# Query and key chunks of a q/k/v projection: five float32r products per weight tile instead of six, with a readout in two halves

## What is computed

```python
def project_qkv(h, w_qkv, q_norm, k_norm):
    b, t, _ = h.shape
    p = (h @ w_qkv).reshape(b, t, N_GROUPS, 3, H_SLOT, HEAD_DIM)
    q = rmsnorm(p[:, :, :, 0], q_norm)
    k = rmsnorm(p[:, :, :, 1], k_norm)
    v = p[:, :, :, 2]
    return q, k, v
```

## Time and profile before

| | before |
|---|---|
| median of three runs | 1206.25 us |
| profiled execution | 1206.42 us |
| its span, first to last instruction | 1204.9 us |
| mean granted TensorE clock | 0.999 of full speed |
| matmul busy (weight loads busy) | 1192.5 us, 99% (1142.0 us, 95%) |
| VectorE busy | 779.7 us, 65% |
| ScalarE busy | 544.1 us, 45% |

### The profile page before, as it was taken

One profiled execution on the slowest core, in us unless ns is written; L12 is line 12 of the kernel. 1 busy time (PEld: TensorE's weight loads), 2 busy tenths in 40 slices (PEclk: granted clock), 3 DMA queues, 4 the chain that ended last, 5 costly groups with the idle time before them and its releaser, 6 DMA issues.

```text
span 1204.9 us, 26364 instructions
## 1 busy us (share of the span) xinstructions
PE 1192.5 (99%) x10349; PEld 1142.0 (95%) x10349; DVE 779.7 (65%) x1427; ACT 544.1 (45%) x953; POOL 21.1 (2%) x50
## 2 busy tenths in 40 slices
PE   8999999999999999999999999999999999999998
PEld 8999999999999999999999999988999999999998
DVE  6766676777776644445686776768877777774333
ACT  5333345445445433224466555555654444542221
POOL 0000000000000000000000000000000000000000
PEclk9999999999999999999999999999999999999999
DMA  8355544656444545455467766668544454546542
GB/s 218 100 164 168 171 119 138 201 152 191 151 135 149 165 155 161 142 170 171 151 209 193 222 181 184 193 168 221 147 149 138 147 173 152 151 144 182 131 115 44
DMA packets 285301, 193.19 MB, mean 160 GB/s; under 512 B 40393, under 2 KB 281537, under 8 KB 284070
## 3 DMA queue, kind: packets, MB, share of 16 engines
q1 hardware_dynamic: 282092, 137.04, 41.5%
q0 software_dynamic: 1792, 54.43, 12.6%
q10 hardware_dynamic: 1338, 0.61, 0.2%
HBM read 184.52 MB, written 64.16 MB: 206 GB/s over the span
## 4 chain that ended last, share of the span: by engine, by line
PE 88%; DVE 7%; ACT 2%; issue 2%; DMA 0%; DVEq 0%; ACTq 0%
PE acc L1968 21%; PE acc L1950 15%; PE acc L1972 11%; PE acc L1969 11%; PE acc L1970 11%; PE acc L1971 11%; DVE wl L1273 1%; PE acc L1998 1%; DVE u L1744 1%; PE N L1937 1%; PE N L2242 1%; PE M L1937 1%; DVE big L1626 1%; ACT wh L872 1%; DVE skv L1737 1%
## 5 line engine op out<-in xcount | busy, mean ns | idle before, releaser
L872 ACT ACTIVATE wh<-wraw 128x1024 fp32r<-128x1024 f32 (+1 forms) x211 | 217.9, 1033 | 267.5 <-PE acc L1972 175.6
L1273 DVE TENSOR_TENSOR wl<-wraw,wh 128x1024 fp32r<-128x1024 f32 (+1 forms) x211 | 252.9, 1199 | 128.9 <-ACT wh L872 100.2
L1968 PE MATMUL acc<-h_both,wh 128*128 128x512 f32 x840 | 319.0, 380 | 2.1 <-DVE wl L1273 1.9
L1972 PE MATMUL acc<-h_both,wl 128*128 128x264 f32 x840 | 233.5, 278 | 0.0
L1970 PE MATMUL acc<-h_both,wh 128*128 128x264 f32 x840 | 231.8, 276 | 0.0
L1969 PE MATMUL acc<-h_both,wh 128*128 128x264 f32 x840 | 231.8, 276 | 0.0
L1971 PE MATMUL acc<-h_both,wl 128*128 128x256 f32 x840 | 229.0, 273 | 0.0
L1970 PEld LDWEIGHTS acc<-h_both,wh 128*128 128x128 f32 x840 | 158.8, 189 | 22.7
L1950 PE MATMUL acc<-h_both,wh 128*128 128x256 f32 x1120 | 173.4, 277 | 0.4 <-DVEq L1678 0.3
L1968 PEld LDWEIGHTS acc<-h_both,wh 128*128 128x128 f32 x840 | 161.3, 192 | 2.7 <-issue 2.2
L1969 PEld LDWEIGHTS acc<-h_both,wh 128*128 128x128 f32 x840 | 158.8, 189 | 0.0
(11 more groups left out here) (274 smaller groups left out, 1735.7 us busy)
## 6 DMA issues: line engine op xcount, KB each, us to landing
out_dram<-in_cache_kv_d_dram POOLq DMA_DIRECT2D x24, 1364.0 KB, 6.2
wraw<-in_ffn_w_gate_dram SPq DMA_DIRECT2D x44, 512.0 KB, 3.9
wraw<-in_ffn_w_up_dram SPq DMA_DIRECT2D x44, 512.0 KB, 3.9
wraw<-in_attn_w_qkv_dram SPq DMA_DIRECT2D x36, 512.0 KB, 4.2
out_dram<-in_cache_kv_d_dram POOLq DMA_DIRECT2D x8, 2044.0 KB, 8.3
wraw<-in_ffn_w_down_dram SPq DMA_DIRECT2D x32, 448.0 KB, 3.9
wraw<-in_sc_w_in_dram SPq DMA_DIRECT2D x24, 512.0 KB, 3.9
wraw<-in_ffn_w_down_dram SPq DMA_DIRECT2D x16, 512.0 KB, 4.3
```

The source lines that it names most:

```text
L872: nc.scalar.activation(wh[c % 2][:, 0:k], wraw[:, c % 4, 0:k], ACT.Copy).then_inc(hi_done, 1)
L1273: V.tensor_tensor(wl[c % 2][:, 0:k], wraw[:, c % 4, 0:k], wh[c % 2][:, 0:k].bitcast(F32), ALU.subtract).then_inc(split_done, 1)
L1968: T.matmul(wide, h[:, k, :], wide_pairs(both[:, :, k0 + k]), start=start, stop=False)
L1972: ins = T.matmul(rest, l[:, k, :], paired(high, 1, CUT), start=False, stop=stop)
```

## The change

Query and key chunks (`c % 3 < 2`, 24 of the 36) use `wide_products`. ScalarE gets a `keep_low` ahead of the split of the next weights, for each of them; it writes the low result straight into the buffer of queries and keys, and waits until the normalisation of the tile that lay there before is done. VectorE's readout first scales the columns of bank 1, then adds part 0 to the kept low result, then scales the samples, releases the banks, and scales the sum only afterwards. Value chunks stay as they were.

```diff
         IN_WIDE = 3 * (DK - 1)
-        WIDE = (IN_WIDE, IN_WIDE + 2 * FK - 4)
+        QKV_WIDE = IN_WIDE + 2 * FK
+        WIDE = (IN_WIDE, QKV_WIDE + 6 * NP_ - 4)
+
+        def prompt_tile(q):
+            return qk_t[:, q % 2, 0:SEQ].rearrange("p (h n) -> p h n", h=2)
...
             for cc in range(9 * NP_):
                 p, c = divmod(cc, 9)
                 n = (p - 1) * NCLS + (c - 1) // 2
+                if cc and (cc - 1) % 3 < 2:
+                    q = (cc - 1) // 9 * 6 + (cc - 1) % 9 // 3 * 2 + (cc - 1) % 3
+                    if q >= 2:
+                        act.wait_ge(norm_ready, q - 1)
+                    keep_low(S_QKV, 0, cc - 1, qkv_bank(cc - 1), prompt_tile(q))
                 if cc:
                     step(S_QKV, 0, cc - 1)
...
                 if c % 3 < 2:
                     q = p * 6 + 2 * g + c % 3
                     t = qk_t[:, q % 2]
-                    V.tensor_tensor(t[:, 0:SEQ].rearrange("p (h b n) -> p h b n", h=2, b=2), prompt_by_half(a),
-                                    cut2(prompt(r)), ALU.mult)
+                    n = QKV_WIDE + q + 1
+                    V.tensor_tensor(rest_set(prompt_tile(q)), rest_part(a)[:, :, 0:CUT], rest_set(prompt(r)), ALU.mult)
+                    dve.wait_ge(low_kept, n)
+                    V.tensor_tensor(wide_set(prompt_tile(q)), wide_part(a, 0), wide_set(prompt_tile(q)), ALU.add) \
+                        .then_inc(set_sum, 1)
                     ch.after(V.tensor_tensor(t[:, SEQ:TT].rearrange("p (h n) -> p h n", h=2), sample_by_half(a),
                                              sample(r), ALU.mult))
+                    dve.wait_ge(set_sum, n)
                     dve.sem_inc(acc_free, 1)
+                    ch.after(V.tensor_tensor(wide_set(prompt_tile(q)), wide_set(prompt_tile(q)), wide_set(r), ALU.mult))
                     dve.sem_inc(qk_ready, 1)
                     return
...
-            def wide_products(st, it, c, par, nk, both, k0, first, last, inserts=None):
+            def wide_products(st, it, c, par, nk, both, k0, first, last, inserts=None, dst=None):
...
-                wide, some, rest = wide_bank(acc[:, par]), pair_bank(acc[:, par], 0, CUT), \
-                    pair_bank(acc[:, par], 1, CUT)
+                dst = acc[:, par] if dst is None else dst
+                wide, some, rest = wide_bank(dst), pair_bank(dst, 0, CUT), pair_bank(dst, 1, CUT)
...
-                products(S_QKV, 0, cc, None, DK, hh, hl, 0, True, True, inserts, CUT, qkv_bank(cc))
+                if c % 3 < 2:
+                    wide_products(S_QKV, 0, cc, None, DK, h_both, 0, True, True, inserts, qkv_bank(cc))
+                else:
+                    products(S_QKV, 0, cc, None, DK, hh, hl, 0, True, True, inserts, CUT, qkv_bank(cc))
```

## The result

The changed kernel takes 1208.93 us (median of 13 runs, 1208.51 to 1209.43) against 1206.12 us for the kernel before (13 runs, 1205.71 to 1206.81): a ratio of 1.0023, 95% interval 1.0015 to 1.0032. It is slower by 2.8 us; the prediction said slower by 3.8. The profiled execution's span is 1207.6 us against 1204.9.

The account below looks back on a forecast made before the run. TensorE's stream was taken as the bound, with VectorE and ScalarE full between chunks 2 and 6 of each pair. 3 x 1.63 = 4.9 us lost, 18 x 0.06 = 1.1 gained: +3.8, 1210.0 us; range 1207.0 to 1212.5.

Parts of the forecast that it names:

- TensorE's part: Six products become five in query and key chunks: 5.38 to 5.32 us, 0.06 us a chunk, 1.4 us at most.
- second rival: Weight loads set TensorE's pace: one load of six gone saves 0.9 us a chunk, 1184.7 us; chance 0.03.
- Unknown costs: ScalarE and VectorE reading two banks of one result at once: between 0 and 0.39 us, taken as 0.
- Step 1: Pairs 1 to 3, chunk 1's end to chunk 3's readout: ScalarE's copy delays ScalarE and VectorE, +0.28 us.
- Step 2: Chunk 3's readout and squares in pairs 1 to 3: the low squares start later, +0.97 us.
- Step 3: Chunk 4's readout in pairs 1 to 3: 0.97 us late and 0.66 longer, +1.63 us at the maxima.
- Step 4: From the maxima through chunk 5 to the value readout: the 1.63 us arrives whole at TensorE's start of chunk 6.
- Some 6 us for the value readout: Sign of being right: TensorE's three waits for the value readout grow from 1.2 to some 6 us.
- three waits under 2 us: Sign of being wrong: TensorE's three waits for the value readout stay under 2 us.
- bank rival: Later bank release stops TensorE at each of 18 chunks of pairs 1 to 3, 0.19 us each: 1208.2 us; chance 0.05.
- Hidden: Longer readouts in pair 0 (six) and at chunks 0, 1, 6 and 7 of pairs 1 to 3 don't stop TensorE.
- the fit into idle time: Longer readouts fit into VectorE's idle time, where normalisations wait 21.9 us for ScalarE: 1204.8 us; chance 0.17.

Follow-up runs that it names:

- x34: Changed kernel, but query/key chunks 3 and 4 of pairs 1 to 3 keep six products and the one-piece readout: 1205.57 us against 1206.01 before.
- x134: Changed kernel, but chunks 1, 3 and 4 of pairs 1 to 3 stay as before, 15 wide chunks left: 1205.04 us, ratio 0.9992.
- only34: Kernel before, with five products only in chunks 3 and 4 of pairs 1 to 3: 1209.39 us, ratio 1.0028.
- moved_after: Changed kernel with the key_sums of the third sample group moved from chunk 4 to behind chunk 5's reciprocals: 1206.49 us against 1206.08 before.
- late_free: Changed kernel with the banks released behind the scaling of the wide set instead of ahead of it: 1210.18 us, ratio 1.0035.
- moved_x4: Changed kernel with the moved sums and only chunk 4 of pairs 1 to 3 with six products, 21 wide chunks: 1205.75 us, ratio 0.9995.
- moved_pool: Changed kernel with the moved sums, all 24 chunks wide, the readout's last scaling on GpSimd instead of VectorE: 1204.71 us, ratio 0.9989.
- moved_x14: Changed kernel with the moved sums and chunks 1 and 4 of pairs 1 to 3 narrow, 18 wide chunks: 1204.23 us, again 1204.79 us.

## Why the prediction was right, point by point

- **TensorE's part** held: 5.32 us a chunk in the stage as in the gate stage. The 18 chunks outside the chain gave 0.06 us each as was taken, 1.05 us against 1.1. That loads are not the pace is now shown in this stage: one of six fewer is worth 0.06 us, not 0.9. The Trainium skill (Perfetto Trace Analysis, Identifying the Most-Contended Engine) judges TensorE's headroom by MFU (the useful share of its peak arithmetic) and by the busy share of weight loads; it does not say that loads set the pace, which is how the prediction's second rival read it. Read so, it does not agree with the trace: the share fell from 95% to 94% only, and the stage did not get a sixth shorter.
- **Unknown costs.** ScalarE and VectorE reading the two banks at once cost nothing: in chunk 3 the copy (624.23 to 624.62) and the readout's first operation (from 624.40) overlap, and the copy takes 0.39 us and the operations start 0.33 apart, against 0.39 and 0.34 one after the other in the earlier trace rows. Where VectorE waits for the chunk, the wait for the copy was sized 0.09 and measured 609.78 - 609.30 - 0.33 = 0.15; it fell on idle time.
- **Step 1** was sized +0.28 and measured +0.26: chunk 3's readout starts 15.10 us after chunk 1's readout, 14.84 before. The reading that this readout starts when VectorE gets to it was incomplete: in the kernel before, chunk 3's end on TensorE and the end of VectorE's normalisation fall together there, in all three pairs. In pair 1 both the split that TensorE releases and the readout start at 624.84. The readout has no room on either side, and so VectorE's lateness shows whole.
- **Step 2** was sized +0.97 and measured +0.82 (low squares 17.95 us after chunk 1's readout starts, 17.13 before). The term that was too large is the squares' release: 1.52 us after the readout's start instead of 1.65.
- **Step 3** was sized +1.63 and measured +1.39 (maxima 24.30 after the same start, 22.91 before). The readout held VectorE 1.60 us, not 1.69: its two hand-overs left 0.18 us each, the lower end of the range given, not the 0.22 taken.
- **Step 4** held: of the 1.39, 1.38 arrive at chunk 6's start. But the stop does not appear under one name: the head sums, which come ahead of chunk 6 on TensorE, wait first for both parts of the squares. "Some 6 us for the value readout" was wrong as a reading: that row grew from 1.2 to 1.5 us only. By the prediction's own sign, three waits under 2 us, this should have told against it; the sign was badly chosen, since the earlier waits take up the lateness. The start of chunk 6 is what shows it.
- **The sum.** The 3 x 1.63 = 4.9 came to 3.86 in all: step 3's and step 2's sizes account for most, and pair 2 lost only 1.14, since its stretch was already 0.2 longer before. With the gain of 1.05 that makes the stage 2.8 us longer, as the medians have it, instead of 3.8. The mechanism stands; these sizes were off. By its number alone the bank rival, with 1208.2, came as near to 1208.9 as the forecast of 1210.0; it is x34, x134 and only34 that tell the two apart.
- **Hidden.** That the six readouts of pair 0 and those of chunks 0, 6 and 7 cost nothing is borne out by x134: 15 wide chunks give the whole 0.065 us each. Chunks 0, 1, 6 and 7 start with no booked wait for a query or key readout; the one such wait is at chunk 4.

Of the rivals, the fit into idle time is out by the trace of after and by moved_after: the idle time in chunk 5 was there, but behind ScalarE, whose wait moved along; it became usable only when other work was moved into it. The bank rival exists in small: chunk 2's first step grew by 0.10 us behind a wide chunk 1, in every kernel that has one (0.76 to 0.78 us in after, x34, late_free, moved_after, moved_x4 and moved_pool, 0.67 in the others). Its readout starts at 609.30, its release by the forecast's 1.06 us falls at 610.36, and chunk 2 starts at 610.43. That the bank is what lengthens this step is argued from that coincidence; no wait is booked there until late_free delays the release. At chunk 4 of pair 1 a wait for the banks is booked (0.15 us); it is covered, for VectorE comes to that chunk's readout only 0.95 us after ScalarE's copy of it (632.00, 631.05). The Trainium skill's rule (Perfetto Trace Analysis, Matmuls) that independent groups should rotate through banks agrees with the rows at chunks 2 and 4, where late_free pays 0.44 and 0.36 us; elsewhere in the pair TensorE's other work does the same service.

## What to carry to other kernels

Find the stretch in which the engine that reads out has no idle time of its own, and price a longer readout only there: six readouts of 24 made the whole loss. An engine that waits on a partner does not offer that wait as slack if the partner waits on it in turn; independent work moved into such a wait does use it. Here moving 1.4 us of sums took 2.4 us off the changed kernel; but 1.1 of these it also takes off the kernel before, so run the move without the edit, too, before crediting either. With the move, the wide product pays a little where the readout has cover: moved_x14 beat both kernels twice (1204.2 and 1204.8 us), and beside it the kernel that has the move alone, by 0.7 us (0.3 the second time, each from its own kernel before). It stands only some 0.15% under the kernel before, less than the bound that the prediction set for a difference.

## What was not expected of the hardware

- An elementwise multiplication on GpSimd slowed VectorE's subtraction: the 128x1024 subtraction took 1.21 to 1.23 us where none ran beside it, and 1.44, 1.53 and 1.59 us where a 128x256 multiplication of GpSimd ran during its first 0.36, 0.45 and 0.51 us. So some 0.15 us less than the overlap was lost each time, and the 24 multiplications that were taken off VectorE (some 0.6 us each with a hand-over) came back in part on its weights. The Trainium skill (GPSIMD Engine Reference, Specifications) says that GpSimd's memory interfaces are shared with VectorE, with contention for VectorE instructions that have two inputs in that memory; the subtraction is one, and the trace agrees.
- A chunk's first step mostly takes 0.67 us where head sums lie directly ahead of it on TensorE, and 0.74 to 0.78 us behind transposes or the attention's logits and values, or after a booked wait, in narrow and wide chunks alike (a few take 0.85 to 0.90). Chunk 2 behind a wide chunk 1, and chunk 8 in late_free, are the exceptions, 0.76 to 0.78 us behind head sums. Where no wait is booked, no row shows what these 0.1 us are.
